# Prompt attention in a decoder trunk: the inverse sums go to the other output bank and stand behind the transposes, and the sample selection's products stand behind the value products

## The chip, the cores and the metric

The kernel runs on one core of one Trainium2 chip. The metric is the device time of one execution in microseconds (us); less is better. Before the change the median of 3 runs is 3053.36 us (3051.23 to 3054.34). The engines that matter here are TensorE (PE in the rows, with PEld for its weight loads), VectorE (DVE), ScalarE (ACT) and GpSimd (POOL). Each runs its own list of instructions in order and waits on semaphores that the others raise.

## What is computed

One layer of a decoder: low-rank attention (MLA) beside an indexer-selected sparse attention (DSA), then a mixture of experts, for a prompt of 1024 tokens and 8 sample sequences. The change lies in the attention over the prompt alone, for both kinds of heads:

```python
s = einsum('qhd,shd->hqs', q, k) * SCALE            # + bias for DSA
s = where(key_pos <= q_pos, s, -inf)                # DSA: also only the 256 selected keys
p = softmax(s, axis=-1)
o = einsum('hqs,shv->qhv', p, v)
```

In the same stretch a second, small piece of work is carried along: for the 8 sample sequences, whose selected 256 of 8193 keys are known as a threshold, it makes the list of selected positions and of cache rows.

## The kernel before

The function `attend` does this stretch. Queries go in 8 tiles of 128 (tile i from 0 to 7). Of one tile, 8 items are done: 4 pairs of heads of the first kind (g = 0), then 4 pairs of the second (g = 1), so 64 items n. Rows of tile i see 128*(i+1) keys. Every item passes through these steps, and each engine's list is written out by hand:

- `scores(n)` (PE, L995): q times k for the two heads, to the four banks `aS`. For g = 1 it waits until both maxima of item n-1 are taken, for g = 0 it takes them one by one.
- `scale_and_max(n)` (DVE, L1147 and L1152): scale, mask, write `S` and the negated row maximum `mx`.
- `exps(n)` (ACT, L1095): exponential in place, with the row sums; `invert(n)` (DVE, L1159): the inverse sums `rs`.
- `turn(n)` (PE, L1012): transposes of the 128x128 blocks of `S`, up to 4 in a group, the groups in turn to the two banks `aT0` and `aT1`; a group waits until the group two before it has been copied out. `evac` copies a group to `PT` (ACT L1078; DVE L1076 for one of the four groups of items from tile 4 on).
- In the list of groups each `turn(n)` is led by one group of another sort (a < 0, L1008): the inverse sums of item n-1, spread over 128 partitions by two products with the identity, also to `aT`. ACT copies it to `RB` (L1078 too, 128x128).
- `pv(n)` (PE, L1050): value products, to bank `aO[n % 2]`, columns 0 to 127.
- `norm(n)` (DVE, L1241): `aO` times `RB`, to `O`, which SP stores once per tile.

PE's list is: scores(n+1), turn(n), pv(n-1). DVE's: scale_and_max(n+1), its part of evac(n), invert(n), norm(n-1), then side work. ACT's: evac(n), exps(n+1).

Side work for the sample selection: `place(k)` (DVE, L1228 and L1230) makes one-hot rows `zA` and `zB` of a chunk k for items 24 to 55 (tiles 3 to 6), after norm(n-1). `values(k)` (POOL, L956 and L957) multiplies `zB` by rows and positions. `pv(CHUNK0 + k)` begins with a wait for that, does 16 or 17 small products (L1037, two PE instructions each) into columns 256 to 287 of `aO`, and then its value products. `read_sums` (DVE, L1213, L1211) adds them up before norm. Items 8, 14, 58 and 62 have other small products in the same place (L1026 to L1046). A second kind of side work, `select` (DVE, L1116 to L1125), runs in the 4 items of g = 1 of tiles 1 to 6: it builds the key mask of the next tile; its second step is a scan.

Of the kernel before, what the change touches and what calls it, by code (L numbers as in the profile page):

```python
# [15 lines left out]
ACT = mybir.ActivationFunctionType  # L16
# [3 lines left out]
P = 128  # L20
# [824 lines left out]
def attend(nc, T, G, sem, sb, ps, U, thr, FIRST, widths, at):  # L845

    c = G["c"]
# [34 lines left out]
    names = ("S", "nm", "P", "T", "evd", "eva", "O", "on", "row", "mb", "rs", "mx", "v", "fin", "bi")  # L882
    s_S, s_nm, s_P, s_T, s_evd, s_eva, s_O, s_on, s_row, s_mb, s_rs, s_mx, s_v, s_fin, s_bi = (sem("at_" + n) for n in names)
# [25 lines left out]
    with nc.Block() as block:  # L909
# [66 lines left out]
        @block.tensor  # L976
        def _(pe):
            def scores(n):
                i, g, p = items[n]
                if g == 0 and p == 0:  # L980
                    pe.wait_ge(s_q[i % 2], 32 * (i // 2 + 1))
                    for x, (a, b) in enumerate(pieces):
                        if a == i:
                            pe.wait_ge(s_kv[x], 32)
                w = widths[i]
                halves = [(z, min(z + 512, w)) for z in range(0, w, 512)]
                if n:
                    pe.wait_ge(s_nm, 2 * n - 1 if g == 0 else 2 * n)
                for a, (z, e) in ([(a, x) for a in range(2) for x in halves] if g == 0 else [(a, x) for x in halves for a in range(2)]):
                    if n and g == 0 and a == 1 and z == 0:  # L990
                        pe.wait_ge(s_nm, 2 * n)
                    h, r = 2 * p + a, slice(64 * a, 64 * a + 64)
                    q = qm[i % 2][0:QK, h, :] if g == 0 else qd[i % 2][r, p, :]
                    k = kmT[0:QK, h, z:e] if g == 0 else kdT[r, p, z:e]
                    m = pe.matmul(pS[a][z // 512][:, 0:e - z], q, k, start=True, stop=True)  # L995
                    if e == w:
                        m.then_inc(s_S, 1)

            def turn(n):

                for x in range(gfirst[n], gfirst[n + 1]):
                    a, b0, cnt, _ = groups[x]
                    if x >= 2:
                        evacuated(pe, x - 1)
                    if a < 0:
                        pe.wait_ge(s_rs, n)
                        for b in range(2):
                            m = pe.matmul(pT[x % 2][64 * b:64 * b + 64, 0:P], rs[:, (n - 1) % 2, b:b + 1].to_broadcast([P, 64]), c("ident"), start=True, stop=True)  # L1008
                    else:
                        pe.wait_ge(s_P, n + 1)  # L1010
                        for b in range(cnt):
                            m = pe.transpose(pT[x % 2][:, b * P:(b + 1) * P], S[n % 2][a][:, (b0 + b) * P:(b0 + b + 1) * P], c("ident"))  # L1012
                    m.then_inc(s_T, 1)

            def pv(n):
                i, g, p = items[n]
                evacuated(pe, gfirst[n + 1])
                if g == 0 and p == 0:
                    for x, (a, b) in enumerate(pieces):
                        if a == i:  # L1020
                            pe.wait_ge(s_vv[x], 32)
                if n >= 2:
                    pe.wait_ge(s_on, n - 1)
                if n == TOTAL01:
                    pe.wait_ge(s_zc, 1)
                    pe.matmul(pO[0][:, 384:388], c("same_half"), zcnt[:, 0, :], start=True, stop=True)  # L1026
                    pe.matmul(pO[0][:, 388:392], c("before_half"), zcnt[:, 1, :], start=True, stop=True)
                elif n == TOTAL2:
                    pe.wait_ge(s_zc, 2)
                    pe.matmul(pO[0][:, 392:396], c("before_half"), zcnt[:, 2, :], start=True, stop=True)  # L1030
                elif 0 <= n - CHUNK0 < len(chunks):
                    k = n - CHUNK0
                    pr, z, e = chunks[k]
                    pe.wait_ge(s_zb, k + 1)
                    for s in range(e - z):
                        u = s % 4
                        m = pe.matmul(pO[n % 2][32 * u:32 * u + 32, 256:288], zA[:, s, :],  # L1037
                                      zB[:, s, :, :].rearrange("p a b -> p (a b)"), start=(s < 4), stop=(s >= e - z - 4))
                    m.then_inc(s_zm, 1)
                elif n == FOLD:  # L1040
                    pe.wait_ge(s_zl, 1)
                    pe.matmul(pO[0][0:32, 384:512], c("fold32"), zparts[:, :, :].rearrange("p n w -> p (n w)"), start=True, stop=True)
                elif n == TURN:
                    pe.wait_ge(s_zi, 32)
                    for a in range(2):
                        pe.transpose(pO[0][:, 384 + 16 * a:400 + 16 * a], zld[a], c("ident")[0:16, 0:16])  # L1046
                for j in range(i + 1):
                    for a in range(2):
                        h = 2 * p + a
                        m = pe.matmul(pO[n % 2][64 * a:64 * a + 64, 0:P], V[g][:, j, h * 64:h * 64 + 64], PT[n % 2][a][:, j, :],  # L1050
                                      start=(j == 0), stop=(j == i))
                m.then_inc(s_O, 1)

            scores(0)
            for n in range(NI + 1):
                if n + 1 < NI:
                    scores(n + 1)
                turn(n)
                if n:
                    pv(n - 1)  # L1060

        def evac(eng, n, dve):
            for x in range(gfirst[n], gfirst[n + 1]):
                if on_dve[x] == dve:
                    a, b0, cnt, _ = groups[x]
                    eng.wait_ge(s_T, x + 1)
                    if a < 0:
                        if n >= 3:
                            eng.wait_ge(s_on, n - 2)
                        dst = RB[(n - 1) % 2][:, :]  # L1070
                    else:
                        if n >= 2:
                            eng.wait_ge(s_O, n - 1)
                        dst = PT[n % 2][a][:, b0:b0 + cnt, :].rearrange("p a q -> p (a q)")
                    if dve:
                        eng.tensor_copy(dst, pT[x % 2][:, 0:cnt * P]).then_inc(s_evd, 1)  # L1076
                    else:
                        eng.activation(dst, pT[x % 2][:, 0:cnt * P], ACT.Copy).then_inc(s_eva, 1)  # L1078

        @block.scalar  # L1080
        def _(act):
# [7 lines left out]
            def exps(n):  # L1089
                w = widths[items[n][0]]  # L1090
                if n >= 2:
                    act.wait_ge(s_rs, n - 1)
                for a in range(2):
                    act.wait_ge(s_nm, 2 * n + a + 1)
                    m = act.activation(S[n % 2][a][:, 0:w], S[n % 2][a][:, 0:w], ACT.Exp, bias=mx[:, n % 2, a:a + 1],  # L1095
                                       accum_out=sm[:, n % 2, a:a + 1])
                m.then_inc(s_P, 1)
            exps(0)
# [1971 lines left out]
```

## Time and profile before

| what | value |
|---|---|
| median of 3 runs | 3053.36 us |
| profiled execution, span | 3055.4 us |
| prompt attention (`attend`) | about 1395 to 1765 us of the span |
| PE busy in it | 327.89 of 370 us |
| DVE, ACT, POOL busy in it | 260.46, 187.71, 73.84 us |

The profiled execution's own time is its span, from the first instruction to the last; it is 2.0 us above the median of the runs. In a row of the timeline stand the start, the length, the engine, the line, the operation, output <- inputs, and in brackets how long the engine had been idle just before and what released it. Two PE instructions are one product of 4-byte numbers. Successive PE instructions overlap, so that a group's length is some 0.07 us more than its distance to the next.

### The profile page before, as it was taken

What the parts mean: (1) busy time and instruction counts of PE and PEld (TensorE: products, weight loads), DVE (VectorE), ACT (ScalarE), POOL (GpSimd) and SP (SyncE); (2) the same over time, 40 slices, a digit from 0 to 9 for tenths busy, and PEclk for the clock granted to TensorE, in tenths of its full rate; (3) what the DMA queues carried; (4) which work ended last, traced back from release to release, by engine and by line L of the source; (5) the groups of instructions that cost most, each with busy time, mean ns of one, the idle gap of its engine ahead of it and who ended that gap; (6) DMA issues with size and microseconds to landing.
All of it is one profiled execution on the core that took longest, in us unless ns stands there. A gap on an engine that the chain in (4) does not pass through costs nothing. (4 is left out here: it accounts for less than half of the span.)

```text
span 3055.4 us, 43569 instructions
## 1 busy us (share of the span) xinstructions
PE 2640.8 (86%) x14542; PEld 1467.7 (48%) x14542; DVE 1516.6 (50%) x3765; ACT 1107.5 (36%) x2376; POOL 371.7 (12%) x415
## 2 busy tenths in 40 slices
PE   4798995859989798987889969797899899999978
PEld 1344443628878687874556634453333333333322
DVE  0256555477878777784787664583111111111116
ACT  0223221448878588773545501221111111111110
POOL 0000000110010010101232131051000000000025
PEclk7899997979999899995899979899999999999988
DMA  9412123532145021206100083207979788897767
GB/s 385 155 60 83 38 74 110 203 106 72 53 154 192 20 86 38 84 1 171 39 26 17 9 266 120 105 28 297 399 277 401 267 322 307 311 339 253 293 236 291
DMA packets 242841, 510.72 MB, mean 167 GB/s; under 512 B 23030, under 2 KB 101056, under 8 KB 235249
## 3 DMA queue, kind: packets, MB, share of 16 engines
q1 hardware_dynamic: 195396, 328.73, 31.1%
q0 software_dynamic: 28352, 126.04, 11.2%
q10 hardware_dynamic: 18932, 53.91, 4.6%
q8 instruction: 89, 1.46, 0.2%
q14 instruction: 72, 0.58, 0.1%
HBM read 630.82 MB, written 87.01 MB: 235 GB/s over the span
## 5 line engine op out<-in xcount | busy, mean ns | idle before, releaser
L2846 PE MATMUL routed_ex_pG<-dispatch_exWG,routed_ex_XT 128*64 128x512 f32 x2048 | 485.2, 617 | 49.3 <-issue 24.8
L1995 DVE TENSOR_REDUCE ssqc<-SQ 128x8 f32<-128x512 f32 x516 | 346.2, 683 | 126.8 <-ACT SQ L1798 113.5
L1709 PE MATMUL eK<-dWkv,LT 128*128 128x256 f32 x1032 | 318.7, 391 | 12.2 <-ACT SQ L1798 11.8
L1712 PE MATMUL eK<-WA,LT 128*128 128x272 f32 x1032 | 329.1, 401 | 0.0
L2938 DVE COPY routed_ex_XT<-routed_ex_pX 128x512 f32<-128x512 f32 x128 | 85.6, 689 | 468.3 <-PE routed_ex_pX L2833 468.2
L1798 ACT ACTIVATE SQ<-eK 128x512 f32<-128x512 f32 x516 | 291.9, 602 | 58.9 <-PE eK L1712 42.9
L549 PE MATMUL in_pp<-ada_Win,in_hT 128*128 128x512 f32 (+1 forms) x640 | 282.0, 599 | 9.8 <-ACT in_pr L463 9.8
L2846 PEld LDWEIGHTS routed_ex_pG<-dispatch_exWG,routed_ex_XT 128*64 128x64 f32 x2048 | 140.3, 141 | 305.7 <-issue 285.5
L2866 PE MATMUL routed_ex_pY<-routed_ex_WD,routed_ex_AT 128*64 128x512 f32 x1024 | 232.2, 595 | 0.0
L1712 PEld LDWEIGHTS eK<-WA,LT 128*128 128x128 f32 x1032 | 202.0, 196 | 29.4 <-DVE numc L1994 0.2
L1709 PEld LDWEIGHTS eK<-dWkv,LT 128*128 128x128 f32 x1032 | 191.1, 197 | 48.2 <-ACT SQ L1798 16.9
L549 PEld LDWEIGHTS in_pp<-ada_Win,in_hT 128*128 128x128 f32 x640 | 123.1, 194 | 158.3 <-issue 158.2
L1753 ACT ACTIVATE ujunk<-W,unb 128x384 bf16<-128x384 int16 (+5 forms) x192 | 169.5, 883 | 13.3 <-DVEq L1817 12.7
L2899 ACT ACTIVATE routed_ex_sg<-routed_ex_pG 128x256 f32<-128x256 f32 x64 | 24.5, 383 | 410.8 <-PE routed_ex_pG L2846 410.8
L2941 DVE TENSOR_TENSOR routed_ex_sg<-routed_ex_sg,routed_ex_pG 128x256 f32<-128x256 f32 x64 | 26.6, 416 | 246.2 <-ACT routed_ex_sg L2899 246.2
L2174 PE MATMUL out_oY<-out_Wo,out_mT 128*128 128x512 f32 x256 | 117.6, 620 | 26.0 <-DMA out_Wo<-in_w_out 16.8
L2866 PEld LDWEIGHTS routed_ex_pY<-routed_ex_WD,routed_ex_AT 128*64 128x64 f32 x1024 | 70.6, 137 | 133.4 <-issue 133.4
L2910 ACT ACTIVATE routed_ex_Y<-routed_ex_pY 128x512 f32<-128x512 f32 x128 | 76.4, 597 | 158.0 <-PE routed_ex_pY L2866 158.0
L1771 ACT ACTIVATE LT<-eT 128x512 f32<-128x512 f32 x168 | 98.2, 585 | 81.8 <-PE eT L1678 81.7
L1095 ACT ACTIVATE S<-S,mx 128x128 f32<-128x128 f32 (+7 forms) x128 | 97.9, 768 | 42.2 <-DVE mx L1152 41.7
L1012 PE MATMUL aT<-K,S 128*128 128x128 f32 x576 | 92.8, 296 | 14.7 <-issue 9.1
L2833 PEld LDWEIGHTS routed_ex_pX<-K,routed_ex_X 128*128 128x128 f32 x512 | 55.0, 142 | 92.4 <-issue 92.4
(546 smaller groups left out, 3760.5 us busy)
## 6 DMA issues: line engine op xcount, KB each, us to landing
dispatch_exWG<-in_w_e_gu SPq DMA_DIRECT2D x132, 2048.0 KB, 18.9
routed_ex_WD<-in_w_e_down SPq DMA_DIRECT2D x132, 1024.0 KB, 13.5
s_yblk<-routed_ex_Y ACTq DMA_DIRECT2D x64, 512.0 KB
ada_Wada<-in_w_ada SPq DMA_DIRECT2D x8, 3072.0 KB, 17.1
s_yblk<-zrows SPq DMA_DIRECT2D x15, 1024.0 KB
ada_Win<-in_w_in ACTq DMA_DIRECT2D x4, 2048.0 KB, 13.8
s_tdT<-in_td SPq DMA_DIRECT2D x8, 832.0 KB
s_h<-out_h ACTq DMA_DIRECT2D x9, 512.0 KB, 2.6
```

The lines of the kernel that those rows point to most:

```text
L549: m = pe.matmul(pp[n % 2][0:R, 0:b - a], hT[t % 2][:, k, 0:R], Win[:, k, a:b], start=(k == 0), stop=(k == KD - 1))
L1012: m = pe.transpose(pT[x % 2][:, b * P:(b + 1) * P], S[n % 2][a][:, (b0 + b) * P:(b0 + b + 1) * P], c("ident"))
L1095: m = act.activation(S[n % 2][a][:, 0:w], S[n % 2][a][:, 0:w], ACT.Exp, bias=mx[:, n % 2, a:a + 1], accum_out=sm[:, n % 2, a:a + 1])
L1709: pe.matmul(pK[kn % 3][:, 512 + z:512 + z + HK], key, Wkv[:, 4:8, 0:NOPE], start=True, stop=True)
L1712: pe.matmul(pK[kn % 3][:, z:z + HK + 16], key, WA[:, pr, :], start=True, stop=True).then_inc(s_KN, 1)
L1753: act.activation(ujunk[:, 0:w], hi16[:, a:a + w] if i < 16 else flat[:, a:a + w], ACT.Sign, bias=nb[:, j:j + 1], accum_out=cu[:, j:j + 1]) ...
L1771: act.activation(LT[u % 3][0:r, 0:cnt * P], pT[0:r, 0:cnt * P], ACT.Copy).then_inc(s_ev, 1)
L1798: act.activation(SQ[kn % 4].rearrange("p (a n) -> p a n", a=2), pK[kn % 3][:, :].rearrange("p (a n) -> p a n", a=2)[:, :, z:z + HK], ACT.S ...
L1995: dve.tensor_reduce(ssqc[cg % 2][:, n - 1 - tau, :], SQ[kn % 4].rearrange("p (h d) -> p h d", h=H), AX.X, ALU.add).then_inc(s_red, 1)
L2174: m = pe.matmul(pY[n][0:R, :], mT[t % 2][:, k, 0:R], Wo[:, k, n * 512:(n + 1) * 512], start=(k == 0), stop=(k == KD - 1))
L2846: m = pe.matmul(pG[u][r, :], XT[u][:, k, r], WG[2 * u + v][:, k, :], start=(k == 0), stop=(k == KD - 1))
L2866: m = pe.matmul(pY[n][r, :], AT[u][:, k, r], WD[2 * u + v][:, k, n * 512:(n + 1) * 512], start=(k == 0), stop=(k == 1))
```

## The change

The inverse sums are no longer a group of `turn`. They are a step of their own, `inverse_sums(n-1)`, behind `turn(n)` and ahead of `pv(n-1)`; they go to columns 128 to 255 of the output bank that `pv(n-1)` does not use, and wait for norm(n-2), which read that bank last. ACT copies them (`take_inverse`) behind its copies of the transposes and ahead of `exps(n+1)`. In `pv(n)` the value products come first, the sample selection's products behind them. In the items with chunks s_O is raised right behind the value products, and `norm` waits for the placement products (s_zm) as well. `invert` and `norm` wait on the new semaphores s_inv and s_inve.

```diff
@@ groups
-        if n:
-            groups.append((-1, 0, 1, -1))
@@ turn, and a new step
+            def inverse_sums(n):
+
+                pe.wait_ge(s_rs, n + 1)
+                if n >= 1:
+                    pe.wait_ge(s_on, n)
+                for b in range(2):
+                    m = pe.matmul(pO[(n + 1) % 2][64 * b:64 * b + 64, P:2 * P], rs[:, n % 2, b:b + 1].to_broadcast([P, 64]), c("ident"), start=True, stop=True)
+                m.then_inc(s_inv, 1)
@@ pv
-                if n >= 2:
-                    pe.wait_ge(s_on, n - 1)
+                for j in range(i + 1):
+                    for a in range(2):
+                        h = 2 * p + a
+                        m = pe.matmul(pO[n % 2][64 * a:64 * a + 64, 0:P], V[g][:, j, h * 64:h * 64 + 64], PT[n % 2][a][:, j, :],
+                                      start=(j == 0), stop=(j == i))
...
                 elif 0 <= n - CHUNK0 < len(chunks):
+                    m.then_inc(s_O, 1)
                     k = n - CHUNK0
                     pr, z, e = chunks[k]
                     pe.wait_ge(s_zb, k + 1)
...
                     m.then_inc(s_zm, 1)
+                    return
...
-                for j in range(i + 1):
-                    for a in range(2):
-                        h = 2 * p + a
-                        m = pe.matmul(pO[n % 2][64 * a:64 * a + 64, 0:P], V[g][:, j, h * 64:h * 64 + 64], PT[n % 2][a][:, j, :],
-                                      start=(j == 0), stop=(j == i))
                 m.then_inc(s_O, 1)
@@ PE's loop
                 turn(n)
                 if n:
+                    inverse_sums(n - 1)
                     pv(n - 1)
@@ ACT
+            def take_inverse(n):
+                act.wait_ge(s_inv, n + 1)
+                if n >= 2:
+                    act.wait_ge(s_on, n - 1)
+                act.activation(RB[n % 2][:, :], pO[(n + 1) % 2][:, P:2 * P], ACT.Copy).then_inc(s_inve, 1)
+
             for n in range(NI + 1):
                 evac(act, n, False)
+                if n:
+                    take_inverse(n - 1)
                 if n + 1 < NI:
                     exps(n + 1)
@@ invert
                 if n >= 2:
-                    dve.wait_ge(s_T, gfirst[n])
+                    dve.wait_ge(s_inv, n - 1)
@@ norm
                 dve.wait_ge(s_O, n + 1)
+                if 0 <= n - CHUNK0 < len(chunks):
+                    dve.wait_ge(s_zm, n - CHUNK0 + 1)
                 read_sums(n)
-                evacuated(dve, gfirst[n + 1] + 1)
+                dve.wait_ge(s_inve, n + 1)
```

TensorE's list in tile 3, one item with heads of the second kind, before: `aS` are scores, `aT` transposes or inverse sums (those from `rs`), `aO` outputs.

```order
L995 MATMUL aS<-kdTs,qdt 128x512 [waits at_nm]
L995 MATMUL aS<-kdTs,qdt 128x512
L1008 MATMUL aT<-K,rs 64x128 [waits at_rs,at_eva]
L1008 MATMUL aT<-K,rs 64x128
L1012 MATMUL aT<-K,S 128x128 [waits at_P,at_eva]
L1012 MATMUL aT<-K,S 128x128 x3
L1012 MATMUL aT<-K,S 128x128 [waits at_P,at_eva]
L1012 MATMUL aT<-K,S 128x128 x3
L1037 MATMUL aO<-zB,zA 32x32 [waits az_rows,at_on,at_eva]
L1037 MATMUL aO<-zB,zA 32x32 x15
L1050 MATMUL aO<-PT,vmS 64x128 x8
```

The same item on TensorE in the change:

```order
L993 MATMUL aS<-kdTs,qdt 128x512 [waits at_nm]
L993 MATMUL aS<-kdTs,qdt 128x512
L1005 MATMUL aT<-K,S 128x128 [waits at_P,at_eva]
L1005 MATMUL aT<-K,S 128x128 x3
L1005 MATMUL aT<-K,S 128x128 [waits at_P,at_eva]
L1005 MATMUL aT<-K,S 128x128 x3
L1014 MATMUL aO<-K,rs 64x128 [waits at_on,at_rs]
L1014 MATMUL aO<-K,rs 64x128
L1027 MATMUL aO<-PT,vmS 64x128 [waits at_eva]
L1027 MATMUL aO<-PT,vmS 64x128 x7
L1043 MATMUL aO<-zB,zA 32x32 [waits az_rows]
L1043 MATMUL aO<-zB,zA 32x32 x15
```

The inverse sums moved from ahead of the transposes to behind them, and the value products moved ahead of the products that wait for POOL's `zB` (az_rows).

ScalarE's list in the same tile, before (`RB` is the copy of the inverse sums, `PT` of the transposes, `S` the exponentials):

```order
L1078 ACTIVATE RB<-aT 128x128 [waits at_on,at_T]
L1078 ACTIVATE PT<-aT 128x512 [waits at_O,at_T] x2
L1095 ACTIVATE S,sm<-S,mx 128x512 [waits at_nm,at_rs]
L1095 ACTIVATE S,sm<-S,mx 128x512 [waits at_nm]
L1078 ACTIVATE RB<-aT 128x128 [waits at_on,at_T]
```

And in the change:

```order
L1076 ACTIVATE PT<-aT 128x512 [waits at_O,at_T] x2
L1100 ACTIVATE RB<-aO 128x128 [waits at_on,at_inv]
L1093 ACTIVATE S,sm<-S,mx 128x512 [waits at_nm,at_rs]
L1093 ACTIVATE S,sm<-S,mx 128x512 [waits at_nm]
L1076 ACTIVATE PT<-aT 128x512 [waits at_O,at_T] x2
```

The copy to `RB` moved from ahead of the copies to `PT` to between them and the exponentials of the next item.

## Rows read from the trace of the kernel before

**Rows 1.** First line of the profile's page.
```profile
span 3055.4 us, 43569 instructions
```

**Rows 2.** Stretches: length, then busy us of each engine, granted PEclk, DMA.
```profile
1395.00:1765.00 370.00, 327.89 (x3410) 211.60 (x3410) 260.46 (x952) 187.71 (x480) 73.84 (x72) 0.90 0.19 48
...
1400.00:1442.00 42.00, 41.69 (x182) 23.99 (x183) 23.00 (x127) 20.25 (x83) 4.51 (x1) 0.50 0.82 208
```

**Rows 3.** Waits, 1395 to 1765: total us, times, longest us.
```profile
ACT RB L1078 <- PE aT L1008: 117.6, 63, 3.6
...
PE aO L1037 <- POOL zB L957: 13.5, 11, 2.5
...
PEld aT L1012 <- ACT RB L1078: 3.3, 15, 0.3
```

**Rows 4.** Timeline, TensorE, first items of tile 3.
```profile
1499.88 0.46 PE L1037 MATMUL aO<-zB,zA 128*32 128x32 f32 x32 [1.49 <-POOL zB L957]
1500.27 1.09 PE L1050 MATMUL aO<-PT,vmS 128*64 128x128 f32 x16
1501.30 1.98 PE L995 MATMUL aS<-kmTs,qmt 96*128 96x512 f32 x4
...
1504.61 0.46 PE L1037 MATMUL aO<-zB,zA 128*32 128x32 f32 x32
...
1509.31 0.46 PE L1037 MATMUL aO<-zB,zA 128*32 128x32 f32 x32 [0.76 <-ACT PT L1078]
```

**Rows 5.** Timeline, VectorE, tile 3: start of `read_sums` in successive items.
```profile
1510.84 0.19 DVE L1213 TENSOR_TENSOR zparts<-zparts,aO 128x32 f32<-128x32 f32 x1 [0.94 <-PE aO L1050]
...
1522.33 0.19 DVE L1213 TENSOR_TENSOR zparts<-zparts,aO 128x32 f32<-128x32 f32 x1 [1.33 <-PE aO L1050]
...
1528.56 0.19 DVE L1213 TENSOR_TENSOR zparts<-zparts,aO 128x32 f32<-128x32 f32 x1 [0.95 <-PE aO L1050]
...
1534.18 0.19 DVE L1213 TENSOR_TENSOR zparts<-zparts,aO 128x32 f32<-128x32 f32 x1 [0.68 <-PE aO L1050]
```

**Rows 6.** Timeline, TensorE, tile 4.
```profile
1545.98 0.46 PE L1037 MATMUL aO<-zB,zA 128*32 128x32 f32 x32 [0.68 <-POOL zB L957]
...
1569.89 0.46 PE L1037 MATMUL aO<-zB,zA 128*32 128x32 f32 x32 [1.42 <-POOL zB L957]
...
1576.60 0.46 PE L1037 MATMUL aO<-zB,zA 128*32 128x32 f32 x32 [1.31 <-POOL zB L957]
1576.99 1.31 PE L1050 MATMUL aO<-PT,vdS 128*64 128x128 f32 x20
```

**Rows 7.** Timeline, VectorE, tile 4: the second maximum of an item, and `read_sums`.
```profile
1570.65 0.15 DVE L1152 TENSOR_REDUCE mx<-mxp 128x1 f32<-128x3 f32 x1
...
1578.35 0.19 DVE L1213 TENSOR_TENSOR zparts<-zparts,aO 128x32 f32<-128x32 f32 x1
```

**Rows 8.** Timeline, tile 5, TensorE and VectorE.
```profile
1623.99 2.83 PE L1050 MATMUL aO<-PT,vdS 128*64 128x128 f32 x24
...
1626.87 0.19 DVE L1213 TENSOR_TENSOR zparts<-zparts,aO 128x32 f32<-128x32 f32 x1 [1.65 <-PE aO L1050]
...
1632.49 1.53 PE L1050 MATMUL aO<-PT,vdS 128*64 128x128 f32 x24
```

**Rows 9.** Timeline, TensorE, tile 6.
```profile
1691.60 1.75 PE L1050 MATMUL aO<-PT,vdS 128*64 128x128 f32 x28
```

**Rows 10.** Timeline, ScalarE, tile 2.
```profile
1474.57 0.28 ACT L1078 ACTIVATE RB<-aT 128x128 f32<-128x128 f32 x1 [0.35 <-PE aT L1008]
...
1477.51 0.28 ACT L1078 ACTIVATE RB<-aT 128x128 f32<-128x128 f32 x1 [0.35 <-PE aT L1008]
```

**Rows 11.** Timeline, TensorE: the last item's transposes, and the inverse sums at two clocks.
```profile
1440.17 0.69 PE L1008 MATMUL aT<-K,rs 128*64 128x128 f32 x4
...
1443.54 0.44 PE L1008 MATMUL aT<-K,rs 128*64 128x128 f32 x4
...
1754.86 1.06 PE L1012 MATMUL aT<-K,S 128*128 128x128 f32 x8 [0.92 <-ACT S L1095]
```

More of the change, by code:

```diff
@@ L881, in attend @@
     pO = [ps("aO0"), ps("aO1")]
-    names = ("S", "nm", "P", "T", "evd", "eva", "O", "on", "row", "mb", "rs", "mx", "v", "fin", "bi")
-    s_S, s_nm, s_P, s_T, s_evd, s_eva, s_O, s_on, s_row, s_mb, s_rs, s_mx, s_v, s_fin, s_bi = (sem("at_" + n) for n in names)
+    names = ("S", "nm", "P", "T", "evd", "eva", "O", "on", "row", "mb", "rs", "mx", "v", "fin", "bi", "inv", "inve")
+    s_S, s_nm, s_P, s_T, s_evd, s_eva, s_O, s_on, s_row, s_mb, s_rs, s_mx, s_v, s_fin, s_bi, s_inv, s_inve = (sem("at_" + n) for n in names)
     s_q, s_out = [sem("at_q0"), sem("at_q1")], [sem("at_o0"), sem("at_o1")]
@@ L1004, in turn @@
                         evacuated(pe, x - 1)
[L1005 to L1012, printed above, removed]
-                    m.then_inc(s_T, 1)
+                    pe.wait_ge(s_P, n + 1)
+                    for b in range(cnt):
+                        m = pe.transpose(pT[x % 2][:, b * P:(b + 1) * P], S[n % 2][a][:, (b0 + b) * P:(b0 + b + 1) * P], c("ident"))
+                    m.then_inc(s_T, 1)
+            def inverse_sums(n):
[5 more added lines that the diff above has]
+                m.then_inc(s_inv, 1)
             def pv(n):
@@ L1026, in pv @@
                     pe.matmul(pO[0][:, 384:388], c("same_half"), zcnt[:, 0, :], start=True, stop=True)
-                    pe.matmul(pO[0][:, 388:392], c("before_half"), zcnt[:, 1, :], start=True, stop=True)
+                    m = pe.matmul(pO[0][:, 388:392], c("before_half"), zcnt[:, 1, :], start=True, stop=True)
                 elif n == TOTAL2:
                     pe.wait_ge(s_zc, 2)
-                    pe.matmul(pO[0][:, 392:396], c("before_half"), zcnt[:, 2, :], start=True, stop=True)
+                    m = pe.matmul(pO[0][:, 392:396], c("before_half"), zcnt[:, 2, :], start=True, stop=True)
                 elif 0 <= n - CHUNK0 < len(chunks):
+                    m.then_inc(s_O, 1)
                     k = n - CHUNK0
@@ L1039, in pv @@
                     m.then_inc(s_zm, 1)
+                    return
                 elif n == FOLD:
                     pe.wait_ge(s_zl, 1)
-                    pe.matmul(pO[0][0:32, 384:512], c("fold32"), zparts[:, :, :].rearrange("p n w -> p (n w)"), start=True, stop=True)
+                    m = pe.matmul(pO[0][0:32, 384:512], c("fold32"), zparts[:, :, :].rearrange("p n w -> p (n w)"), start=True, stop=True)
                 elif n == TURN:
@@ L1045, in pv @@
                     for a in range(2):
-                        pe.transpose(pO[0][:, 384 + 16 * a:400 + 16 * a], zld[a], c("ident")[0:16, 0:16])
-                for j in range(i + 1):
-                    for a in range(2):
-                        h = 2 * p + a
-                        m = pe.matmul(pO[n % 2][64 * a:64 * a + 64, 0:P], V[g][:, j, h * 64:h * 64 + 64], PT[n % 2][a][:, j, :],
-                                      start=(j == 0), stop=(j == i))
+                        m = pe.transpose(pO[0][:, 384 + 16 * a:400 + 16 * a], zld[a], c("ident")[0:16, 0:16])
                 m.then_inc(s_O, 1)
@@ L1066, in evac @@
                     eng.wait_ge(s_T, x + 1)
[L1067 to L1074, printed above, removed]
+                    if n >= 2:
+                        eng.wait_ge(s_O, n - 1)
+                    dst = PT[n % 2][a][:, b0:b0 + cnt, :].rearrange("p a q -> p (a q)")
                     if dve:
@@ L1097, in exps @@
                 m.then_inc(s_P, 1)
+            def take_inverse(n):
+                act.wait_ge(s_inv, n + 1)
+                if n >= 2:
+                    act.wait_ge(s_on, n - 1)
+                act.activation(RB[n % 2][:, :], pO[(n + 1) % 2][:, P:2 * P], ACT.Copy).then_inc(s_inve, 1)
             exps(0)
```

## Prediction

> **What bounds the kernel now.** I read the page's first part, then the stretch of prompt attention in the table of stretches, then its waits, then its timeline item by item. The whole span is 3055.4 us [rows 1]. The changed code is one stretch of 370 us, and there TensorE is busy for 328 us, VectorE for 260, ScalarE for 188 [rows 2]. The rest of the kernel is separate stages that start when this one has ended, so what it gains or loses goes to the end whole. TensorE's list is the chain. Its idle time in the stretch is 42 us, and the waits say where the change can reach: TensorE's placement products (L1037) waited 11 times, 13.5 us in all, for GpSimd's `zB`, and its weight loads for transposes waited 15 times, 3.3 us in all, for ScalarE's copy of the inverse sums to `RB` [rows 3]. The reader is to see in the timeline that at each such gap the value products, which need nothing of `zB`, stand right behind the waiting products: 1.49 us idle, then L1037, then L1050 for 1.03 us up to the next scores [rows 4]. The other idle time (the wait for the stage's first keys, a short gap between two groups of transposes in tiles 4 to 7, waits for maxima in tiles 1 and 2) isn't touched.
>
> **Part 1: the inverse sums leave the transposes' banks.** The same two products per item are issued, 64 times, and the same 64 copies on ScalarE, so nothing is removed. In tiles 0 and 1 an item has two groups of transposes; the second shared its bank with the inverse sums and waited for the copy to `RB`: 3.3 us over 15 items, 0.22 each [rows 3]. That wait goes. Some of these items are held by VectorE's maxima (late in tile 1), where TensorE's gain is lost. Bounds 0 and 3.3 us; I take 2.3, ten or eleven items' worth. From tile 4 on there are four groups, and the idle between the second and the third is a wait for the copy of a first group, which starts and ends with the transposes as before: 0.
>
> It adds a wait: the inverse sums wait for norm(n-2), where before the value products waited for norm(n-3). Behind the waiting instruction stand the value products, and VectorE waits for these. But norm(n-2) begins as soon as the products of item n-2 are done and takes half a us with `read_sums`, while TensorE does the scores and transposes of a whole item before it asks; where VectorE is late, exps(n), which the transposes need, is later still than the start of that norm. 0, with 0.3 us an item in two or three items as upper end: 1 us.
>
> ScalarE's copy to `RB` comes behind its copies of the transposes and ahead of the next exponentials. Its wait for the inverse sums before is 117.6 us over 63 items [rows 3], 1.87 in the mean, so in nearly all items the 0.28 us of the copy fall into slack. The narrowest slack is in tile 2, heads of the second kind: 0.35 us [rows 10]. There transposes start 0.37 us earlier relative to the scores, since the inverse sums no longer precede them, but the copy of 0.28 us is in ScalarE's loop from transposes to exponentials to the next transposes. From one copy to `RB` to the next are 2.94 us, TensorE's time for an item, of which ScalarE idles 0.35 ahead of the copy; the other 2.6 now have the first group of transposes in front of them, which used to run beside that copy, some half a us (8 transposes take 1.06 [rows 11]): 3.1 us, an estimate. 0.15 us lost in three items, 0.5 us. Bounds 0 and 0.28 us in the 8 items of the tile, 2.2 us.
>
> At the end the last item's transposes wait 0.92 us for their exponentials [rows 11]; the inverse sums ahead of them lay in that wait, now they stand behind it: 0.3 us lost (they last 0.39 to 0.44).
>
> **Part 2: the value products ahead of the placement products.** What is gained at a gap is the shorter of the gap and the value products, and it is kept only as far as VectorE keeps pace.
>
> Tile 3. First gap: 1.49 us against value products of 1.03 (1501.30 - 1500.27) [rows 4]: 1.03 gained. From then on VectorE and TensorE take turns: VectorE makes `zA`, GpSimd multiplies, TensorE places, then does value products, and VectorE waits for these before `read_sums`: 0.94 us in the item at 1510.84 and in the next, then 1.33, 0.95, 0.68 [rows 5]. With the value products done earlier, `read_sums` needs only the placement products, which end while VectorE is still at the maxima. An item then takes the longer of VectorE's work and TensorE's. In the first two, TensorE's: 4.70 us less the gap of 0.76, 3.94 (1509.31 - 1504.61) [rows 4], so 0.76 is gained in each; in the other three VectorE's, so its wait is gained: 1.33 + 0.95 + 0.68. Sum 4.5, with the first 5.5 us.
>
> Tile 4. A gap of 0.68 at 1545.98 is covered whole: 0.7 us. The two gaps of 1.42 and 1.31 belong together [rows 6]. Between them VectorE has no wait at all: in the timeline it works through from before the second maximum at 1570.65 up to `read_sums` at 1578.35 [rows 7]. So `zB` of the second gap is ready when it was, and what was gained at the first is waited for there (the next scores need that second maximum too). Only one length of value products is kept: 1.31 less 0.07 of overlap, 1.2 us.
>
> Tile 6 has the same pair (gaps of 1.2 us twice), and keeps 1.75 less 0.07, 1.7 us [rows 9].
>
> Tile 5. VectorE did wait in this pair: 1.65 us for value products that ran 2.83 us instead of the 1.53 of the same products later [rows 8], because the granted clock was down at 1.2 GHz. VectorE's wait goes, 1.65, and the second gap keeps one length of value products, 1.5: 3.1 us, of which 1.3 is the clock's and stays lost if the clock falls again.
>
> Sum of part 2: 5.5 + 0.7 + 1.2 + 1.7 + 3.1 = 12.2 us. Bounds: below, only VectorE's waits in rows 5, which must vanish (3.9 us); above, the 13.5 us of rows 3, the two gaps of 0.76 that the profile puts down to ScalarE, and the clock's 1.3: 16 us. A granted clock isn't in the order of instructions, so I put half a drop in tile 5 back: 0.7.
>
> `read_sums` gets a second wait and the other small products (items 8, 14, 58, 62) move behind the value products; VectorE needed both kinds before too, and the sum of their lengths is unchanged: 0.
>
> **The sum.** 2.3 - 0.5 - 0.3 + 12.2 - 0.7 = 13.0 us. The profiled execution would go from 3055.4 to 3042.4. It stands 2.0 us above the median of the runs, so the median goes from 3053.4 to 3040.4; I say 3040.
>
> **A rule beside it.** The rows show TensorE at a granted clock of 0.50 (1.2 GHz) in the first 42 us of the stretch, in which it always had work [rows 2]. The Trainium skill, "TensorE: Matmul & The Clock Gate", Part 1, says that the default state is throttled and that activity releases it. By that rule denser items could raise the clock sooner than in the trace, a result of its own, which is the first rival below. The trace bears it out in part only: work without a break for 42 us left the clock where it was, until tile 1.
>
> **The rivals.**
> A. The clock. The inverse sums take 0.69 us at 1.2 GHz and 0.44 at 2.4 GHz [rows 11], so 10 us of the slow stretches at the higher clock save some 3.6 us. With the waits of 0.22 us gone from tiles 0 and 1, the clock could rise sooner: 42 us are slow [rows 2], and half of them regained is 8 us more. For it: the rise came in tile 1, as scores got wider. Against: most of that stretch has no idle time in it to take away. Time 3053.4 - 13 - 8, about 3032.
> B. The gaps come back elsewhere. In tiles 3 to 6 VectorE is the one that is late; TensorE may meet it at the next maximum instead of at `zB`. Then only the surely vanishing 3.9 us and half of part 1 stay: gain 4 to 5, time 3049, no measurable change. For it: the pairs in tiles 4 and 6, where half is lost so. Against: VectorE's own waits for L1050 in rows 5, which can't exist if it is saturated.
> C. Slower: ScalarE's loop. If the copy to `RB`, now between the transposes' copies and the exponentials, delays every item's exponentials, and TensorE waits for them at each next turn, then 63 times 0.28 us are lost, 17.7, and the gaps' gain goes into the same waits: 3071. It decides from the point where ScalarE's slack ahead of the copy (1.87 in the mean, 0.35 at the narrowest) is below 0.28 us plus what transposes and exponentials need to hand over. The mean speaks against it, tile 2 shows that it isn't far.
> D. The change doesn't do what it says: the inverse sums wait for norm(n-2) in many items. 0.3 us in 50 items would eat the gain: 3055.
>
> **Chances.** The forecast 0.72, with its own range 3036 to 3045; A 0.12; B 0.11; C 0.03; D 0.02. The range for the time reaches from A's middle to B's: 3033 to 3048. What a measurement of this kernel can tell from no change is 0.2%, 6 us, so faster means under 3047.3: the forecast and A, and a little of B: 0.86. Within 0.2%: most of B and some of D, 0.11. Slower: C and the rest, 0.03.
>
> **What will show it.** In the profile of the changed kernel: no wait of weight loads for transposes on the copy to `RB`; placement products that wait in four or five items instead of 13, and under 5 us in all (the second of each pair in tiles 4 to 6, and one or two in tile 3); VectorE's waits ahead of `read_sums` in tile 3's last items gone; the scores of tile 4 starting some 7 us sooner than before, counted from the stretch's first scores, and those of tile 7 some 13 us. Waits of transposes for exponentials only in tile 2 and at the end. The prediction is wrong if transposes wait for ScalarE's exponentials in tiles 3 to 7, if the inverse sums wait for norm, or if the scores of heads of the second kind wait for maxima as long as L1037 waited before. If the time moves by more than 20 us, the row to look at is the granted clock from the stretch's start to tile 2.

## The result and the profile after: 28 us less, where 13 were forecast

Median 3025.8 us of four runs, beside 3053.9 us for the kernel before: ratio 0.991, 95% interval 0.9897 to 0.9924, 28.1 us less. The direction was right; the time lies below the range of 3033 to 3048. The page's first line, against [rows 1]:

```profile
span 3026.0 us, 43539 instructions
```

The stretches (columns as in [rows 2]: length, busy us of each engine with counts, granted PEclk, DMA):

```profile
1400.00:1425.00 25.00, 23.04 (x120) 16.08 (x122) 16.81 (x98) 13.83 (x61) 4.51 (x1) 0.57 1.10 267
1425.00:1460.00 35.00, 29.09 (x250) 19.60 (x248) 29.84 (x121) 22.62 (x79) 4.54 (x1) 0.99 0.39 92
...
1395.00:1731.00 336.00, 292.58 (x3410) 205.23 (x3410) 262.13 (x952) 184.18 (x480) 73.87 (x72) 0.96 0.21 53
```

The same 3410 instructions now take 292.6 us of TensorE, not 327.9. Idle time explains none of the gain: it is 43 us, where it was 42. The products themselves became shorter. The granted clock is full from 1425 on, where in [rows 2] it was half up to 1442. Before, it then fell back to half from 1450 to 1466, with TensorE busy all the time, and for 3.4 us each in tiles 3 and 5 (from 1521 and from 1624); in the changed kernel no such fall is left before the last item ends. Here is that stretch of the kernel before:

```profile
1450.00:1466.00 16.00, 16.00 (x65) 8.95 (x64) 9.01 (x34) 6.90 (x23) 4.51 (x1) 0.50 0.18 41
```
 The waits after the change, against [rows 3] (total us, times, longest us):

```profile
PE aS L993 <- DVE mx L1158: 10.9, 15, 1.8
...
PE aO L1043 <- POOL zB L955: 5.5, 7, 1.6
...
PE aT L1005 <- ACT S L1093: 2.7, 7, 1.1
...
PE aO L1014 <- DVE O L1249: 1.1, 1, 1.1
```

The wait of transposes for `RB` is gone, that for `zB` fell from 13.5 us to 5.5, and waits for maxima came instead. In the timeline of TensorE the first gap of tile 3 [rows 4] stayed nearly as long, 1.42 us, but the value products are already done and the next scores follow at once; in tile 4 [rows 6] the next wait is for a maximum:

```profile
1483.98 0.46 PE L1043 MATMUL aO<-zB,zA 128*32 128x32 f32 x32 [1.42 <-POOL zB L955]
1484.37 1.98 PE L993 MATMUL aS<-kmTs,qmt 96*128 96x512 f32 x4
...
1545.91 0.46 PE L1043 MATMUL aO<-zB,zA 128*32 128x32 f32 x32 [0.33 <-POOL zB L955]
1546.97 1.35 PE L993 MATMUL aS<-kdTs,qdt 64*128 64x512 f32 x8 [0.61 <-DVE mx L1158]
```

Of VectorE's waits ahead of `read_sums` that [rows 5] show in tile 3, 0.68 to 1.33 us each, 0.17 us in one item are left; the item ahead of them still waits 0.82 us:

```profile
1489.01 0.19 DVE L1219 TENSOR_TENSOR zparts<-zparts,aO 128x32 f32<-128x32 f32 x1 [0.82 <-PE aO L1043]
...
1496.66 0.19 DVE L1219 TENSOR_TENSOR zparts<-zparts,aO 128x32 f32<-128x32 f32 x1 [0.17 <-PE aO L1043]
...
1507.26 0.19 DVE L1219 TENSOR_TENSOR zparts<-zparts,aO 128x32 f32<-128x32 f32 x1
```

So much was looked for. What was not is in an item without any wait. Tile 7, a head of the first kind, before and after (start, us, line, product):

```profile
1718.50 3.70 PE L995 MATMUL aS<-kmTs,qmt 96*128 96x512 f32 x8
1722.13 0.44 PE L1008 MATMUL aT<-K,rs 128*64 128x128 f32 x4
1722.50 1.12 PE L1012 MATMUL aT<-K,S 128*128 128x128 f32 x8
...
1724.93 1.97 PE L1050 MATMUL aO<-PT,vmS 128*64 128x128 f32 x32
1726.83 1.56 PE L995 MATMUL aS<-kdTs,qdt 64*128 64x512 f32 x6
```

```profile
1684.17 3.70 PE L993 MATMUL aS<-kmTs,qmt 96*128 96x512 f32 x8
1687.71 1.04 PE L1005 MATMUL aT<-K,S 128*128 128x128 f32 x8
...
1690.09 0.44 PE L1014 MATMUL aO<-K,rs 128*64 128x128 f32 x4
1690.36 1.92 PE L1027 MATMUL aO<-PT,vmS 128*64 128x128 f32 x32
1692.21 1.99 PE L993 MATMUL aS<-kdTs,qdt 64*128 64x512 f32 x8
```

The same products last 8.33 us from scores to scores before and 8.04 after. Read starts, not durations: from the inverse sums to what follows are 0.37 us in the one and 0.27 in the other, and the scores give way to the next products (inverse sums before, transposes now) after 3.63 us in the one and 3.54 in the other. At 1.2 GHz, in tile 1, it is more. Before and after:

```profile
1420.45 2.08 PE L995 MATMUL aS<-kmTs,qmt 96*128 96x256 f32 x4
1422.45 0.69 PE L1008 MATMUL aT<-K,rs 128*64 128x128 f32 x4
1423.08 0.92 PE L1012 MATMUL aT<-K,S 128*128 128x128 f32 x2
...
1424.55 2.08 PE L995 MATMUL aS<-kmTs,qmt 96*128 96x256 f32 x4
```

```profile
1418.22 2.08 PE L993 MATMUL aS<-kmTs,qmt 96*128 96x256 f32 x4
1420.09 0.64 PE L1005 MATMUL aT<-K,S 128*128 128x128 f32 x2
1420.65 0.69 PE L1014 MATMUL aO<-K,rs 128*64 128x128 f32 x4
...
1421.70 2.08 PE L993 MATMUL aS<-kmTs,qmt 96*128 96x256 f32 x4
```

4.10 us against 3.48. In front_other_bank below, which has the old order without the wait for `RB`, this item lasts 3.87 us; so 0.23 of the 0.62 goes to that wait and 0.39 is left to the order.

### The profile page after: what moved, and what is told of

It is laid out like the page before. It is cut to its first block and busy times, and to the rows that moved or that the text cites. A ratio compares the mean times of both kernels' runs of the same rounds, so it can differ in the third digit from the quotient of the medians.

```text
span 3026.0 us, 43539 instructions
## 1 busy us (share of the span) xinstructions
PE 2603.9 (86%) x14542; PEld 1460.3 (48%) x14542; DVE 1517.6 (50%) x3765; ACT 1104.7 (37%) x2376; POOL 370.1 (12%) x415
## 5 line engine op out<-in xcount | busy, mean ns | idle before, releaser
L1717 PEld LDWEIGHTS eK<-dWkv,LT 128*128 128x128 f32 x1032 | 191.0, 197 | 48.2 <-ACT SQ L1806 17.0
L1076 ACT ACTIVATE PT<-aT 128x128 f32<-128x128 f32 (+3 forms) x160 | 68.5, 467 | 113.0 <-PE aT L1005 113.0
```

The lines of the kernel that those rows point to most:

```text
L1717: pe.matmul(pK[kn % 3][:, 512 + z:512 + z + HK], key, Wkv[:, 4:8, 0:NOPE], start=True, stop=True)
```

## The experiments

Where the time goes is read from tile lengths: from a tile's first scores to those of the next, in the timeline; the last ends with the last norm. The last column says when the granted clock first rose to 1.00 for more than 5 us, and where it was back at 0.50 before tile 7. Tile lengths and clocks are of one profiled execution of each kernel, the medians are of all its runs.

| kernel | median us | stretch | tiles 0, 1, 2 | tile 3 | 4 | 5 | 6 | 7 | clock up, and half again |
|---|---|---|---|---|---|---|---|---|---|
| before | 3053.9 | 362.0 | 20.7, 33.2, 33.3 | 41.6 | 49.8 | 55.7 | 59.3 | 68.5 | 1443; 1450 to 1466, 1521 to 1525, 1624 to 1627 |
| changed | 3025.8 | 328.2 | 18.4, 25.4, 27.5 | 36.0 | 45.7 | 51.1 | 56.0 | 68.2 | 1425 (and 1408 to 1412) |
| p1_inverse_only | 3046.1 | 353.5 | 18.8, 25.4, 31.5 | 44.2 | 50.7 | 55.0 | 59.2 | 68.8 | 1425; 1442 to 1456, 1490 to 1497, 1514 to 1517, 1562 to 1565, 1623 to 1626 |
| p2_values_first | 3041.4 | 346.7 | 20.7, 31.5, 32.3 | 36.4 | 47.0 | 52.5 | 57.6 | 68.7 | 1439; 1450 to 1463 |
| front_other_bank | 3038.7 | 347.7 | 19.3, 32.8, 32.3 | 36.4 | 46.9 | 52.6 | 57.6 | 69.8 | 1442; 1449 to 1463 |
| inverse_in_gap | 3020.2 | 323.5 | 18.7, 25.5, 27.5 | 36.0 | 45.1 | 49.8 | 54.7 | 66.3 | 1425 |
| inverse_behind | 3037.6 | 343.4 | 20.7, 26.9, 29.1 | 36.7 | 46.6 | 52.0 | 56.9 | 74.4 | 1429 |
| inverse_split | 3048.6 | 355.7 | 21.8, 33.2, 31.1 | 37.0 | 48.2 | 53.8 | 59.0 | 71.7 | 1444; 1454 to 1461 |

**Each part alone.** p1_inverse_only is the changed kernel with `pv` as it was:

```diff
-                for j in range(i + 1):   # value products first
+                (placement, count and fold products)
+                for j in range(i + 1):   # value products last
```

> Only the first half of the change: inverse sums behind the transposes, in the other output bank; the placement products stay ahead of the value products. Theory (order and clock): TensorE's own time for an item falls by about 0.3 us in items of the first kind and 0.15 in those of the second, and the granted clock rises in tile 1 some 15 us sooner; both hang on this half. Then the stretch (362.0 us before, 328.2 in the change) comes to about 338, the run 20 to 25 us below before, and TensorE waits for zB 13 times as before. Rival (the gaps carry it, as the prediction had it): no more than 3 us below before.

p2_values_first is the kernel before with only the new order in `pv`; the inverse sums stay ahead of the transposes.

> Only the second half: value products ahead of the placement products; the inverse sums stay a group of turn, ahead of the transposes. Theory (order and clock): only the gaps at the placement products go, 8 to 12 us, and the clock rises at about 1443 us as before. Rival (the gaps carry it, and the clock follows from them): 20 us or more below before. In either case the copy to RB still holds the second group of transposes in tiles 0 and 1.

Ratios 0.9968 (0.9958 to 0.9979) and 0.9953 (0.9935 to 0.9971): by the medians 7.8 and 12.5 us less, 20 in sum where both together give 28. By the intervals the parts may also add up to the whole. p1 missed its expectation (20 to 25 us less, a stretch of 338 us); p2 came near its own (8 to 12 us less). p2 gains 5.1, 2.8, 3.2 and 1.7 in tiles 3 to 6, 12.8 us, where the forecast had 12.2. Not all of that is gaps: the falls of the clock in tiles 3 and 5 are gone in p2 as well. The first gap is covered, in its timeline too, against [rows 4] and [rows 5]:

```profile
1497.76 0.46 PE L1043 MATMUL aO<-zB,zA 128*32 128x32 f32 x32 [0.37 <-POOL zB L957]
```

```profile
1516.31 0.19 DVE L1215 TENSOR_TENSOR zparts<-zparts,aO 128x32 f32<-128x32 f32 x1
```

p1 has the early clock and the short tiles 0 and 1, and loses much of it again in tiles 2 to 4, where the clock fell four times (two of the stretches):

```profile
1440.00:1455.00 15.00, 13.71 (x60) 8.83 (x62) 9.53 (x38) 6.56 (x21) 3.29 (x1) 0.57 0.19 44
...
1490.00:1500.00 10.00, 10.00 (x82) 5.92 (x80) 5.12 (x16) 3.37 (x9) 1.66 (x3) 0.66 0.00 0
```

Tile 3 is 2.6 us longer than before: it has the old gaps and 10 us at the half clock. In the changed kernel neither is there. In the profiles the parts take 8.5 and 15.3 us off the stretch and both together 33.9; of the missing 10 us some 8 lie in tiles 2 to 4. This rests on one profile of each kernel, and that of p1 is its slowest execution of ten, 10.9 us above their median.

**The bank, without the new place.** The changed kernel with inverse sums and copy ahead of the transposes again, in the other output bank:

```diff
+                if n:
+                    inverse_sums(n - 1)
                 turn(n)
-                if n:
-                    inverse_sums(n - 1)
```

> The whole change, but the inverse sums (in the other output bank) and ScalarE's copy of them stand ahead of the transposes, as before. Theory (neighbours): the distance from the inverse sums to what follows them is 0.37 us again (0.27 in the change), items of the first kind lose their 0.3 us again, and the run is 8 to 15 us slower than the change; the second group of transposes in tiles 0 and 1 doesn't wait for the copy. Rival (the bank and the freed wait count, not the place): within 3 us of the change.

Ratio 0.9945 (0.9928 to 0.9962), no better than p2 by more than the intervals allow. Only the bank differs from p2 here. At 1.2 GHz an item of tile 0 lasts 3.02 us, in p2 3.26; this is the wait of [rows 3]: 0.23 per item, 1.4 us in tile 0, 0.23 in the first item of tile 1, and nothing behind it (4.31 us for the next item, 4.32 before). The clock came up at 1442 (timeline; inverse sums 0.69, then 0.44):

```profile
1441.83 0.69 PE L1014 MATMUL aO<-K,rs 128*64 128x128 f32 x4
...
1444.26 0.44 PE L1014 MATMUL aO<-K,rs 128*64 128x128 f32 x4
```

So the bank is worth 1 to 2 us, and the place of the inverse sums the other 13 of the changed kernel's lead over front_other_bank.

**The new waits for maxima.** Scores of the second kind wait for the item's first maximum only, as those of the first kind:

```diff
-                    pe.wait_ge(s_nm, 2 * n - 1 if g == 0 else 2 * n)
+                    pe.wait_ge(s_nm, 2 * n - 1)
-                    if n and g == 0 and a == 1 and z == 0:
+                    if n and a == 1 and z == 0:
```

> The change, and in heads of the second kind the scores of the first head wait for the first maximum only (in the change for both). Theory: the scores' waits for maxima in the change (PE 10.9 us in 15 waits) shrink by about half a us at each of some ten places, 3 to 5 us less time than the change, since VectorE then gets its scores sooner. Rival: VectorE is saturated at these places, the wait comes back at the second head or at the exponentials, and the time is the change's within 1 us.

Ratio 0.9897 (0.9879 to 0.9915), 3024.4 us, tiles as in the changed kernel within 0.3 us. The expectation, 3 to 5 us less than the changed kernel, isn't met: 1.4, well within the intervals. The wait was halved:

```profile
PE aS L993 <- DVE mx L1158: 5.5, 6, 1.5
```

None of TensorE's other waits grew for it; instead TensorE counts as busy for 298.4 of 328 us, where it was 292.4, and every tile is as long as before. The items end no sooner, so this wait wasn't worth removing. That VectorE sets their pace is the likely reason; it wasn't tested by itself.

**A clock raised beforehand.** Before (and, in after_warmed, the changed kernel) with 17 products of constants while TensorE waits for the first keys:

```diff
+            for x in range(17):
+                pe.matmul(pS[x % 2][x // 2 % 2][:, :], c("ident"), K512, start=True, stop=True)
             scores(0)
```

> The kernel before, with 17 products of constants (128x512) on TensorE while the stretch waits for its first keys; their output isn't read. Theory (the clock is a cause of its own): the clock is at 2.4 GHz when the first scores start, stays there for some or all of tiles 0 and 1, and takes 5 to 15 us off these tiles (53.9 us before) and off the whole run. Rival (the clock only follows the density of the items that run): it falls back within one or two items, and the run is within 2 us of before.

> The change, with the same 17 products. Theory (clock): tile 0, which the change runs mostly at 1.2 GHz in 18.4 us, and the first items of tile 1 take 3 to 6 us less; the distance to before_warmed is then what order and gaps are worth without the clock, 17 to 22 us. Rival (the clock follows the items): within 2 us of the change.

Ratios 1.0 (0.999 to 1.001) and 0.9908 (0.9893 to 0.9923): nothing in the time, though the clock was up as the stretch began. Timeline of before_warmed:

```profile
1385.43 17.57 PE L1056 MATMUL aS<-K 128*128 128x512 f32 x34 [2.71 <-PEq L1574]
1402.84 0.61 PE L996 MATMUL aS<-kmTs,qmt 96*128 96x128 f32 x4
...
1412.59 0.44 PE L1009 MATMUL aT<-K,rs 128*64 128x128 f32 x4
...
1414.96 0.69 PE L1009 MATMUL aT<-K,rs 128*64 128x128 f32 x4
...
1419.89 2.08 PE L996 MATMUL aS<-kmTs,qmt 96*128 96x256 f32 x4
```

Twelve us into the items it fell, and rose at 1442 as without it. Tile 0 did get shorter, 17.05 us instead of 20.7. But the 17 products outlasted the wait for the first keys, and the first scores came at 1402.84 instead of 1399.72: the 3.1 us lost there ate up the 3.7 gained. Fewer products, done before the keys land, were not tried. So the clock of the first 12 us came from what ran before, and that of the rest of tiles 0 to 2 was the same as without it.

**Which half of the bank first.** The changed kernel with the halves of the inverse sums in the other order:

```diff
-                for b in range(2):
+                for b in (1, 0):
```

> The change, with the two products of the inverse sums in the other order: upper half of the partitions (b = 1) first, lower half last; the value products still begin with the lower half. Theory A (the freed time is a weight load for one half of the array's columns while the other half computes): the last inverse product and the first value product now share a half, the distance from inverse sums to value products goes from 0.27 back to 0.37 us, value products stay 0.05 longer, and an item of tiles 3 to 7 takes 0.15 us more, some 5 us in these tiles. Theory B (what counts is that both loads have 64 columns, against transposes' 128): 0.27 us stay, same time as the change.

3027.7 us, ratio 0.992 (0.9903 to 0.9936). The distances are the same, 0.26 and 1.85, so theory A, which wanted 0.37, falls:

```profile
1690.32 0.44 PE L1014 MATMUL aO<-K,rs 128*64 128x128 f32 x4
1690.58 1.92 PE L1027 MATMUL aO<-PT,vmS 128*64 128x128 f32 x32
1692.43 1.99 PE L993 MATMUL aS<-kdTs,qdt 64*128 64x512 f32 x8
```

**Changes of tile shape.** The trace writes a product's shape as rows*columns: scores of the first kind 96*128, transposes 128*128, scores of the second kind 64*128, inverse sums and value products 128*64. inverse_behind puts the inverse sums behind the value products; inverse_split one half ahead of the transposes, one beside the value products.

```diff
-                    inverse_sums(n - 1)      # ahead of pv
+                inverse_sums(n)              # in pv, behind the value products
```

```diff
+                if n:
+                    inverse_sums(n - 1, (0,))
                 turn(n)
                 if n:
-                    inverse_sums(n - 1)
+                    inverse_sums(n - 1, (1,))
```

> The changed kernel with the inverse sums issued behind the value products of their item (and ahead of placement products), so that value products now stand behind the transposes and the inverse sums ahead of the next scores. Theory M (a price per change of tile shape): the products of an item come in the shapes 128x128 (scores of g=0, transposes), 64x128 (scores of g=1) and 128x64 (inverse sums, value products), and each change of shape from one group to the next costs TensorE 0.15 us at 2.4 GHz. An item of g=0 had 4 changes before and 2 in the changed kernel (8.33 and 8.03 us in tile 7), one of g=1 4 and 3 (6.62 and 6.47). Here the counts are 2 and 3 as in the changed kernel: the items of tile 7 last 8.03 and 6.47 us again, although every neighbour of the inverse sums but one is another, and the distance from the inverse sums to the next scores is 0.37, not 0.27. The Trainium skill, 'TensorEngine Tiling (Array Packing)', section 'Key Properties', says that changing the tiling mode drains TensorE; it gives no price. Rival N (it is the value products behind the inverse sums that make these short, whatever the shapes): items back at 8.33 and 6.62. Time: ScalarE's copy and so its exponentials come up to 1.9 us later in an item, so transposes may wait for them; 3022 to 3035 us.

> The changed kernel with the first of the two inverse sums' products ahead of the item's transposes, and the second where the change puts both, beside the value products. Same number of products, same banks, same copies. Theory M: 4 changes of shape per item again, for g=0 and g=1: the items of tile 7 last 8.33 and 6.62 us, all that the order of products gave is gone, although half of the inverse sums still stands beside the value products. The distance from the second half to the value products stays some 0.14 (half of 0.27). Rival N (each product of the inverse sums is short when value products follow): half of the gain stays, 8.18 and 6.55. The clock in tiles 0 to 2, by both: below the changed kernel's density, so the rise comes later than 1426, and the time is near that of the kernel with the whole inverse sums ahead of the transposes, 3038.7; 3034 to 3041 us.

Tile 7 of inverse_behind, timeline:

```profile
1685.40 3.70 PE L993 MATMUL aS<-kmTs,qmt 96*128 96x512 f32 x8
1688.93 1.04 PE L1005 MATMUL aT<-K,S 128*128 128x128 f32 x8
...
1691.32 1.97 PE L1027 MATMUL aO<-PT,vmS 128*64 128x128 f32 x32
1693.12 0.39 PE L1012 MATMUL aO<-K,rs 128*64 128x128 f32 x4
1693.43 3.70 PE L993 MATMUL aS<-kmTs,qmt 96*128 96x512 f32 x8
```

8.03 us, as theory M said, with other neighbours on both sides; the rival's 8.33 falls. The distance to the next scores is 0.31 us, not the 0.37 of the expectation. Its 6.47 for the second kind can't be read: these items last 7.32 us here, with a wait of 0.81 for the exponentials in them. Tile 7 of inverse_split:

```profile
1710.57 3.70 PE L993 MATMUL aS<-kmTs,qmt 96*128 96x512 f32 x8
1714.20 0.43 PE L1014 MATMUL aO<-K,rs 128*64 128x128 f32 x2
1714.56 1.09 PE L1005 MATMUL aT<-K,S 128*128 128x128 f32 x8
...
1719.10 1.99 PE L993 MATMUL aS<-kdTs,qdt 64*128 64x512 f32 x8
```

8.53 us and, for the second kind, 6.82: all of the gain gone, as M said, and 0.20 more than its 8.33 and 6.62. Most of that is in one row: half of the inverse sums takes 0.36 us between scores and transposes, as much as both halves. Between two changes of shape it isn't the products that are paid for. The median, 3048.6 (0.9982, 0.9968 to 0.9996), is worse than the 3034 to 3041 expected. inverse_behind's time (3037.6 us, ratio 0.9956, 0.9939 to 0.9972), above the 3022 to 3035 expected, shows another thing: ScalarE's copy, now 1.8 us later in the item, delays the exponentials, and transposes wait for them 17.3 us in 29 times, where they waited 2.7. That is the mechanism of the prediction's rival C.

**Better kernels.** heads_apart with, from tile 4 on, the inverse sums between second and third group of transposes, where TensorE stood 0.30 us in each item, and their copy ahead of that of the last group:

```diff
+                    if in_gap(n) and x == gfirst[n] + 2:
+                        inverse_sums(n - 1)
```

> heads_apart, and from tile 4 on the inverse sums stand between the second and the third group of transposes, where the change leaves TensorE idle for 0.3 to 0.6 us, and ScalarE copies them ahead of the last group's copy. Theory (neighbours): they cost 0.37 us there instead of 0.27 and the value products 0.05 more, but lie in the gap, so an item of tiles 4 to 6 gets 0.2 us shorter and one of tile 7 0.1 to 0.15: 5 to 7 us less than the change. Rival (the gap is a wait for ScalarE's copy, which the extra copy of RB delays by 0.28 us, or the maxima bind): within 2 us of the change.

> inverse_in_gap with the 17 products. If the two gains are separate, 8 to 12 us less than the change, near 3015; if the clock follows the items, the same as inverse_in_gap.

> inverse_in_gap, and the inverse sums of the last item go to a transposes' bank, so that they needn't wait for norm of the item before (1.10 us in the change). 1 us less than inverse_in_gap, near 3019; against the change 5 to 7 us less. If the gain in the stretch is given back in later stages, nothing to be seen beyond inverse_in_gap.

The items of tile 7 fall from 8.04 to 7.82, although the shape now changes twice more: the idle time pays for it. 3020.2, 3020.8 and 3019.6 us; ratios 0.9897 (0.9881 to 0.9913), 0.9887 (0.987 to 0.9904) and 0.9888 (0.9871 to 0.9904). gap_and_tail, the last item's inverse sums in a bank that is free, takes 1.2 us off tile 7. The three can't be told apart by their times.

> The change once more, on the same chip as the two others. Theory (clock follows the items): its profile shows the clock's rise before 1430 us and no fall in tile 2 again, and a stretch of 326 to 331 us. Rival (chance of that one profile): rise at 1440 or a fall in tile 2, and a stretch of 335 us or more.

The changed kernel again: 3022.1 us, 0.99 (0.9884 to 0.9917), stretch 325.6, clock up at 1415 already, which makes tile 1 2.8 us shorter than in its first profile. The three better kernels lead it by 2 to 6 us in the medians, and the intervals overlap. Their gain shows in the tiles: 4, 5, 6 and 7 of inverse_in_gap are 0.6, 1.3, 1.3 and 1.9 us shorter, at the same clock.

## Why the prediction was wrong

**The step that failed** is the first of part 1: "The same two products per item are issued, 64 times, and the same 64 copies on ScalarE, so nothing is removed." The number of products is the same, the changes of shape between them aren't. Counted by the shapes in the trace, with 96*128 and 128*128 taken as one, an item of the first kind had four changes and has two, one of the second kind four and three (placement products add one in either order). At 2.4 GHz they last 0.30 and 0.15 us less, 0.15 per change; at 1.2 GHz 0.39 for two. inverse_behind kept the counts and the length, inverse_split brought four back and lost all, and 0.20 us more, which a price per change alone doesn't give. The Trainium skill, "TensorEngine Tiling (Array Packing)", Key Properties, says that changing the tiling mode, not just the tile, drains TensorE. These runs agree that a change costs time, and give the price that the page doesn't; it was the rule to weigh here. The order is worth 5.3 us in tiles 3 to 7 (changed kernel against p2: 0.5, 1.2, 1.4, 1.6, 0.5); a tile has only eight items, some of them held by VectorE.

**The clock**, rival A at 0.12, came, and larger than its 8 us; this is the bigger part of what the sum missed. Tiles 0 to 2 take 71.3 us instead of 87.2: 15.9 less, where the terms of part 1 had 1.8. Rival A counted the 42 us of [rows 2] as slow and half of them as regained. The trace had 17 us more at 1.2 GHz in tiles 1 and 2, from 1450 on; the time at half clock in the three tiles fell from 60 us to 22. By the prediction's 3.6 us per 10 that is worth some 13.5 us, an estimate. The prediction did name the granted clock as the row to look at should the time move by more than 20 us. Ahead of that rise TensorE is busy 41.7 of 42 us in [rows 2] and 5.00 of 5 in the changed kernel, so the busy share doesn't tell the two apart, and "no idle time in it to take away" was no argument. Every kernel with two or three changes of shape per item came up between 1415 and 1430, every one with four between 1439 and 1444 and fell back for 7 to 18 us soon after. That is an observation on all kernels whose tiles 0 to 3 were run with either count, not a mechanism: ahead of the rise, fewer changes also made the items of tile 1 shorter (3.5 and 3.9 us in inverse_behind, 4.1 and 4.3 before), and no run separates the two. What the clock answers to stays open, also why it fell in p1. How the 15.9 us divide between clock, order and VectorE's pace can't be read, since they act on the same items.

**Point by point.** The gaps: 12.2 forecast, 12.8 measured alone. That this is so close is in part luck: the forecast didn't count the fall of the clock in tile 3 (3.4 us at half, some 1.2 us by the same estimate), which is gone in p2 too. Half a drop put back in tile 5 (0.7): no drop was there. The wait for `RB`: gone, 1.6 us for 2.3. ScalarE's loop in tile 2 at the narrowest slack [rows 10]: the loss came, 0.21 us three times for the 0.15 forecast (timeline),

```profile
1458.59 0.85 PE L1005 MATMUL aT<-K,S 128*128 128x128 f32 x6 [0.21 <-ACT S L1093]
```

and more of it in tiles 0 and 1, where no loss was forecast: 0.27, 0.38 and 0.37 us, the last two at the full clock that came early. The end: inverse sums wait 1.1 us for norm, once, where 0.3 was forecast; this also is the only place of rival D. Placement products wait 5.5 us in 7 places; forecast were under 5 in four or five. Rival B fell.

**The profile gains more than the runs.** The stretch is 33.9 us shorter, the median 28.1. Past it nothing was changed, but the routed experts' stage lasts 837.9 us in the profile before and 845.2 after. Over all 15 profiles it takes either 837 to 838 or 841 to 845, with no relation to the kernel, and the traces show what goes with it: in the seven short ones the granted clock is at half for 37 to 39 us of the stage, in the eight long ones for 42 to 52. Why it falls more often in some executions is open. So the premise of the prediction, "what it gains or loses goes to the end whole", held for each profile only within these 7 us.

## What to carry to other kernels

List TensorE's products by the shape in the trace and count the changes from one to the next; where a small product can stand beside others of its shape, move it there, unless it can fill a gap that stays. Compare starts, since durations of neighbours hide this. Where a stretch runs at half the granted clock, price a denser order at either level before calling it free.

## What the runs showed that was not expected

- A change of shape costs 0.15 us at 2.4 GHz and 0.2 at 1.2; a group of one or two small products between two changes lasts 0.36 to 0.37 either way.
- TensorE busy 41.7 of 42 us stayed at 1.2 GHz, and a clock that had risen during 17.6 us of wide products fell after 12 us of small items.
- Two edits worth 7.8 and 12.5 us alone gave 28.1 together by the medians, and in the profiles 8.5 and 15.3 us against 33.9 of the stretch; the times alone don't exclude a plain sum.
- The length of a stage that no kernel here touched moved by 7 us with the time that the granted clock was at half in it.
